# A hybrid decoder layer on one core: second expert list by column tiles, state-space copies on ScalarE and GpSimd, output projection begun in the gated unit

## The chip, the cores and the metric

The kernel runs on one core of a Trainium2 chip. The metric is the device time of one execution in microseconds (us), the median of several runs; one further execution was profiled. The engines are TensorE (PE, its weight loads PEld), VectorE (DVE), ScalarE (ACT), GpSimd (POOL) and the queue engine SyncE (SP).

## The reference

One layer works on 1024 prompt rows and 8 sample rows of width 1024: a modulated RMS norm, an input projection, then two branches side by side (gated delta rule with four heads, and a diagonal complex state space, "S5", with 32 groups of 16 channels and 64 states), one output projection over both, and a grouped top-2 mixture of 16 experts. What matters here, cut down:

```python
y, x_new = s5_scan(u, x0_s5, ...)            # x_t = Lbar x_{t-1} + Bbar u_t,  y_t = Re(C x_t) + D u_t
y = gelu(y)
y = y * sigmoid(y @ glu_w + glu_b)           # the gated unit
o_b = rms_norm(y, s5_norm_g)
out = concatenate([o_a, o_b], -1) @ w_out    # o_a: delta rule, 512 columns; o_b: 512 columns
x = x + gt1 * out
hn = rms_norm(x, norm2_g) * (1 + sc2) + sh2
# every row goes to two of 16 experts
act = silu(hn @ w_gate[e]) * (hn @ w_up[e]) * combine
x = x + gt2 * (act @ w_down[e])
```

## The kernel before

Every engine runs its own list of instructions, written out by hand; semaphores order them. `X.did(ins, name)` counts a step of engine X and `X.wait(eng, name)` lets another engine wait for it. A wait holds all that is behind it on its engine. The work goes through blocks; three of them are touched.

*State space* (pools `pe`, `act`, `dve`, `pool`, loops `for q in range(4)`, 8 groups in each quarter). The sequence is cut into chunks of 8 steps. For each quarter TensorE transposes the inputs V (`turn_rows`, to banks 2 and 3), the decode inputs (`turn_decode`) and the table W (step `BM`), makes the lag kernel K (step `K`, banks 4 and 5) and the state inputs (step `b`, from BM, BS and U, into banks 0 to 3). ScalarE copies U, Ud, BM and BS out of PSUM. VectorE builds the tables W, CL and CS (`tables`), copies K to Kt, adds the diagonal D to its lag 0 (`dd`), rotates the state inputs by the phases Ec and Es (L1767, step `rot`), runs the scan over chunks (L1826) and rotates back (step `zc`). GpSimd's part in a quarter is one addition to each half of zin, between rotation and scan. SP writes Kt eight times, shifted, into the block Toeplitz matrix TT (L1584); the output matmuls (step `yp`) wait for TT and `zc`. The modulation matmuls (`ada`) run between, in the banks of K.

*Gated unit and output projection*. `glu_tensor` transposes the nine row tiles of y, multiplies by glu_w (steps `glu0` to `glu8`, L1899; the ninth tile has 8 rows), and transposes the normed result (`turned`, L1889), which VectorE evicts into rows 4 to 7 of hT (`evict`, L1954). At i = 7 and 8 three of these transposes stand ahead of or behind a `glu` group. Six row transposes (`rowP`, L1910) are copied by ScalarE. Then the projection (L2648) goes over nine tiles in the order ORDER, two halves of 512 columns each, eight steps k of 128 in each half; steps 0 to 3 read the delta-rule half of hT, which is there since the block before. Routing of an earlier tile is placed between its matmuls (`route_T`, `route`).

*Experts*. Rows are sorted into slices of 64 for one expert; a tile holds two slices (LANES), which may belong to two experts. Expert 0 always has at least two slices. Three weight buffers are filled in turn, as soon as an expert is done (`moe_sync`); a fourth takes ScalarE's and VectorE's copy of the second lane's weights (`gate_up_copy`, `down_copy`). Which rows tile 1 takes is found by comparison (`hit1` on VectorE) and 18 products of the hits with the row numbers, summed in one PSUM column (`who1`, L2260; a float32 matmul is two instructions). GpSimd then gathers the rows (L2127). Tile 0's list (`who`, `who0`) is made earlier.

## Time and profile before

| | us |
|---|---|
| median of 3 runs (lowest, highest) | 1144.13 (1140.65, 1144.68) |
| the profiled execution, its own time | 1146.18 |
| its span in the trace | 1144.3 |
| TensorE busy | 1032.5 (90%) |
| VectorE busy | 582.6 (51%) |
| ScalarE busy | 355.6 (31%) |
| GpSimd busy | 222.8 (19%) |

Busy time is summed over the whole span; it doesn't say in which stage an engine is the one that the others wait for. Matmuls are pipelined, and their ends are modelled. In the lines of the trace, L1899 is line 1899 of the kernel, `out<-in` names the tiles, and a bracket tells how long the engine was idle before the instruction and what ended that.

### The profile page before, as it was taken

The page shows a single profiled execution, that of the slowest core. Times are in us where ns is not written, and L with a number is a line of the kernel's source. Part 1 is how long each engine was busy: PE and PEld are TensorE (multiplying, and loading weights), DVE is VectorE, ACT ScalarE, POOL GpSimd, SP SyncE. Part 2 cuts the span into 40 slices and gives each one's busy share as a digit, 9 for nine tenths or more (in the row PEclk, how much of TensorE's full clock was granted, in tenths as well). Part 3 has the DMA queues.
Part 4 walks back from the last instruction along what each step waited for, and adds up shares of the span by engine and source line. Part 5 has one row for each costly group of instructions (what it writes and reads, how often), then busy time and mean ns, then how long its engine had stood idle before and what let it go on. Part 6 is the DMA issues. An engine that isn't in the chain of part 4 may idle for free. (4 is left out here: it accounts for less than half of the span.)

```text
span 1144.3 us, 15471 instructions
## 1 busy us (share of the span) xinstructions
PE 1032.5 (90%) x5430; PEld 608.5 (53%) x5430; DVE 582.6 (51%) x1289; ACT 355.6 (31%) x723; POOL 222.8 (19%) x361
## 2 busy tenths in 40 slices
PE   3899999899999889969998889999669999999975
PEld 3466666444686777757886335344343333333332
DVE  3243436777236845669981432447653233332238
ACT  6121221115311454333223423332303333332333
POOL 0100000078150444320111000002132111111060
PEclk9899999899999887979988999999859999999988
DMA  9595434202000700058653510131527867699383
GB/s 334 191 241 197 194 115 179 74 38 88 28 13 26 150 2 1 2 178 284 202 199 131 221 74 19 61 106 38 173 67 262 305 229 260 227 352 360 119 316 133
DMA packets 126930, 177.07 MB, mean 155 GB/s; under 512 B 37406, under 2 KB 81683, under 8 KB 126840
## 3 DMA queue, kind: packets, MB, share of 16 engines
q1 hardware_dynamic: 117510, 147.03, 38.2%
q0 software_dynamic: 6432, 18.96, 4.7%
q10 hardware_dynamic: 2906, 10.02, 2.2%
q8 instruction: 47, 0.77, 0.3%
q14 instruction: 35, 0.29, 0.1%
HBM read 129.06 MB, written 45.85 MB: 153 GB/s over the span
## 5 line engine op out<-in xcount | busy, mean ns | idle before, releaser
L371 PE MATMUL bank<-hw 128*128 128x344 f32 x576 | 171.0, 459 | 3.8 <-ACT hw L555 3.8
L371 PEld LDWEIGHTS bank<-hw 128*128 128x128 f32 x576 | 110.6, 193 | 62.6 <-issue 6.4
L2215 PE MATMUL bank<-hw,H 128*64 (+1 forms) x608 | 135.7, 599 | 3.7 <-ACT hw L2293 2.2
L456 PE MATMUL bank<-hw 128*128 128x512 f32 x256 | 115.6, 609 | 4.3 <-ACT qkvT L583 4.3
L2648 PE MATMUL bank<-hw 128*128 128x512 f32 x256 | 116.8, 601 | 0.5 <-DVE hw L1954 0.5
L2215 PEld LDWEIGHTS bank<-hw,H 128*64 128x64 f32 x608 | 44.0, 139 | 91.4 <-issue 89.4
L456 PEld LDWEIGHTS bank<-hw 128*128 128x128 f32 x256 | 64.6, 256 | 51.0 <-issue 32.7
L2293 ACT ACTIVATE hw<-hw 128x2048 f32 (+1 forms) x21 | 40.0, 1909 | 127.2 <-PE bank L2215 92.9
L2233 PE MATMUL bank<-yy,H 128*64 128x512 f32 (+1 forms) x304 | 71.1, 611 | 2.1 <-ACT H L2272 2.1
L2648 PEld LDWEIGHTS bank<-hw 128*128 128x128 f32 x256 | 46.3, 190 | 49.8 <-issue 47.2
L2316 DVE COPY H<-bank 128x256 f32<-128x256 f32 x19 | 8.1, 424 | 113.7 <-PE bank L2198 113.7
L2127 POOL DMA_INDIRECT H<-h_d,small_room x20 | 21.3, 1065 | 193.6 <-DMA yy<-in_w_down 78.8
L577 ACT ACTIVATE pre<-bank 128x344 f32<-128x344 f32 x36 | 13.9, 459 | 122.9 <-PE bank L371 122.9
L915 DVE SCALAR_TENSOR_TENSOR qkvT<-pre,vecT,qkvT 128x1024 f32<-128x1024 f32 x36 | 46.0, 1279 | 0.0
L2432 PE MATMUL bank<-hw 128*128 128x512 f32 (+1 forms) x72 | 35.0, 635 | 8.7 <-DMA hw<-ys_d,pos 5.3
L2565 POOL DMA_INDIRECT ids_d<-small_room x18 | 18.3, 1017 | 124.4 <-DVE small_room L2834 103.9
L2233 PEld LDWEIGHTS bank<-yy,H 128*64 128x64 f32 x304 | 20.6, 139 | 39.1 <-issue 39.1
L908 DVE COPY tail<-pre 128x11 f32<-128x11 f32 x12 | 2.1, 173 | 71.1 <-ACT pre L577 71.0
L1899 PE MATMUL bank<-H,yy 128*128 128x512 f32 (+1 forms) x72 | 33.4, 625 | 0.3 <-DMA H<-in_s_glu_b 0.3
L700 POOL MEMSET V<- 128x8 f32 x2 | 0.2, 110 | 170.3 <-DVE V L892 170.3
L2293 ACT ACTIVATE yy<-yy 128x1024 f32 (+1 forms) x19 | 20.1, 1057 | 40.0 <-PE bank L2233 40.0
L2867 DVE TENSOR_TENSOR H<-bank,V 128x512 f32<-128x512 f32 x16 | 11.0, 690 | 36.5 <-PE bank L2648 36.5
(560 smaller groups left out, 1828.5 us busy)
## 6 DMA issues: line engine op xcount, KB each, us to landing
ys_d<-ZO SPq DMA_DIRECT2D x18, 1024.0 KB, 13.0
yy<-in_w_down SPq DMA_DIRECT2D x16, 1024.0 KB, 10.1
hw<-in_w_gate SPq DMA_DIRECT2D x16, 1024.0 KB, 7.1
hw<-in_w_up SPq DMA_DIRECT2D x16, 1024.0 KB, 10.6
ys_d<-H ACTq DMA_DIRECT2D x19, 512.0 KB, 6.3
hw<-in_w_in SPq DMA_DIRECT2D x4, 2048.0 KB, 8.1
yy<-in_w_ada SPq DMA_DIRECT2D x4, 2048.0 KB, 8.8
hw<-in_w_ada SPq DMA_DIRECT2D x8, 1024.0 KB, 12.1
```

Of the source, the lines that this page charges most:

```text
L371: mm = t.matmul(ps[3 * (m % 2) + s][:, 0:SEG], w_ring[:, q % 2, k, (m % 4) * P:(m % 4 + 1) * P], hT[:, k, s * SEG:(s + 1) * SEG], start=(k ...
L456: mm = t.matmul(ps[b % 4][0:n, :], tok, w_ring[:, q % 2, k, :], start=(k == 0), stop=(k == KD - 1))
L577: act.did(a.activation(pre[:, m % 2, 3 + s * SEG:3 + (s + 1) * SEG], ps[3 * (m % 2) + s][:, 0:SEG], ACT.Copy), f"pre{m}")
L915: dve.did(v.scalar_tensor_tensor(out=y, in0=pre[:, m % 2, i:i + SEQ], scalar=taps[i], in1=y, op0=ALU.mult, op1=ALU.add), f"conv{m}")
L1899: mm = t.matmul(ps[2 + i % 2][0:n, :], y1T[:, k, i * P:i * P + n], glu_w[:, k, :], start=(k == 0), stop=(k == 3))
L2127: g.indirect_dma_start(xin[s % 2][:, :], None, h2_d, bass.IndirectOffsetOnAxis(ap=who[s % 2][:, 0:1], axis=0)).then_inc(x_in[s % 2], 16)
L2215: mm = t.matmul(ps[2 + p][lane, :], xT[p][:, k, lane], wgu[:, bass.ds(bufs[j], 1), k, :].rearrange("p o n -> p (o n)"), start=(k == 0), st ...
L2233: mm = t.matmul(ps[5 + half_][lane, :], aT[s % 2][:, k, lane], wdn[:, bass.ds(bufs[j], 1), k, half_ * 512:(half_ + 1) * 512].rearrange("p ...
L2293: copy = lambda out, in_: a.activation(out, in_, ACT.Copy)
L2432: mm = t.matmul(ps[(5, 2)[i % 2] + half_][:, :], diag[0:n, i % 2, j, :], ya[i % YA][0:n, j, half_ * 512:(half_ + 1) * 512], start=(j == 0) ...
L2565: g.indirect_dma_start(ids_d, bass.IndirectOffsetOnAxis(ap=spot[0:n, i, j:j + 1], axis=0), ids[0:n, i:i + 1], None).then_inc(scat, 16)
L2648: mm = t.matmul(ps[b][:, :], hT[:, k, i * P:(i + 1) * P], w_out[:, k, cols], start=(k == 0), stop=(k == KD - 1))
```

## The change

Three edits. (1) State space: the two copies of K to Kt go from VectorE to ScalarE (new step `Kt`), the addition of the diagonal goes to GpSimd, which makes `dd` once for all groups; all that waited for VectorE's step `K` now waits for GpSimd's. In the first quarter ScalarE copies U as soon as the rows are transposed (new step `rows`), and TensorE does the state inputs (`state_inputs`) ahead of K. (2) Gated unit: `delta_half` does steps k = 0 to 3 of the first three half tiles of the projection in banks 0, 1 and 2, behind `glu7`, `glu8` and `G8`; the projection then goes on with k = 4 for these. (3) Experts: tile 0 takes expert 0's weights from buffer 0 for both lanes, and the copies for it go away; its transposes stand ahead of the second list; the list is made with the row numbers as weights (32 columns wide, the same number in each) on four column tiles and the hits as 128 moving columns, copied by ScalarE, and summed over the four by one more matmul.

```diff
@@ -1559,6 +1559,7 @@
         zl = t4("zl", [P, 2, GROUPS])
+        dd = t4("dd", [CH, GROUPS, CH])
         xrow = t4("xrow", [P, 2, P])
@@ -1575,7 +1576,7 @@
-                    dve.wait(sp, f"K{q}")
+                    pool.wait(sp, f"K{q}")
                     if q == 0:
@@ -1606,8 +1607,12 @@
                 pool.did(g.memset(zs[:, :, 0:1], 0.0), "clear")
+                pool.did(g.tensor_tensor(dd[:, :, :], bc(ident[0:CH, 0:CH], [CH, GROUPS, CH], 1), bc(D16[:, :], [CH, GROUPS, CH]), ALU.mult))
                 for q in range(4):
                     gs, Es = slice(q * NG, (q + 1) * NG), Es2[:, q % 2]
+                    act.wait(g, f"Kt{q}")
+                    pool.drain(g)
+                    pool.did(g.tensor_tensor(Kt[:, :, 0, :], Kt[:, :, 0, :], dd[:, gs, :], ALU.add), f"K{q}")
                     for bnk in range(2):
@@ -1623,8 +1628,9 @@
                     for x in range(NG):
-                        t.transpose(ps[2 + x // 4][:, (x % 4) * P:(x % 4 + 1) * P],
-                                    V[:, q * NG + x].rearrange("p j c -> p (j c)"), ident[:, :])
+                        mm = t.transpose(ps[2 + x // 4][:, (x % 4) * P:(x % 4 + 1) * P],
+                                         V[:, q * NG + x].rearrange("p j c -> p (j c)"), ident[:, :])
+                    pe.did(mm, f"rows{q}")
@@ -1646,6 +1652,15 @@
+                def state_inputs(q):
+                    act.wait(t, f"U{q}")
+                    for x in range(NG):
+                        if x % 4 == 0:
+                            act.wait(t, f"BM{q}_{x // 4}")
+                        t.matmul(ps[x // 4][:, (x % 4) * P:(x % 4 + 1) * P], BM[:, x, :], U[:, x, :], start=True, stop=True)
+                        mm = t.matmul(ps[2 + x // 4][:, (x % 4) * P:(x % 4 + 1) * P], BS[:, x, :], U[:, x, :], start=True, stop=True)
+                    pe.did(mm, f"b{q}")
+
                 turn_rows(0)
@@ -1655,6 +1670,7 @@
                         turn_decode(0)
+                        state_inputs(0)
                     else:
@@ -1662,13 +1678,8 @@
                     pe.did(mm, f"K{q}")
-                    act.wait(t, f"U{q}")
-                    for x in range(NG):
-                        if x % 4 == 0:
-                            act.wait(t, f"BM{q}_{x // 4}")
-                        t.matmul(ps[x // 4][:, (x % 4) * P:(x % 4 + 1) * P], BM[:, x, :], U[:, x, :], start=True, stop=True)
-                        mm = t.matmul(ps[2 + x // 4][:, (x % 4) * P:(x % 4 + 1) * P], BS[:, x, :], U[:, x, :], start=True, stop=True)
-                    pe.did(mm, f"b{q}")
+                    if q > 0:
+                        state_inputs(q)
                     dve.wait(t, "x0")
@@ -1684,7 +1695,7 @@
                         act.wait(t, f"yp{q - 1}")
-                    dve.wait(t, f"K{q}")
+                    pool.wait(t, f"K{q}")
                     if q == 0:
@@ -1699,7 +1710,7 @@
                     dve.wait(t, f"zc{q}")
-                    dve.wait(t, f"K{q}")
+                    pool.wait(t, f"K{q}")
                     t.wait_ge(tt_land, 16 * LAGS * (q + 1))
@@ -1724,11 +1735,12 @@
                 for q in range(4):
-                    pe.wait(a, f"U{q}")
+                    pe.wait(a, f"rows{q}")
                     if q > 0:
 ...
                         act.did(a.activation(U[:, 4 * bnk:4 * bnk + 4, :], ps[2 + bnk][:, :].rearrange("p (g n) -> p g n", g=4), ACT.Copy))
+                    pe.wait(a, f"U{q}")
                     act.did(a.activation(Ud[:, :, :, :].rearrange("p g v b -> p (g v b)"), ps[6][:, P:P + 2 * NG * DEC], ACT.Copy), f"U{q}")
@@ -1739,6 +1751,11 @@
                         act.did(a.activation(BS[:, part, ST:P], src[:, :, 0:ST], ACT.Copy, scale=-1.0), f"BM{q}_{bnk}")
+                    pe.wait(a, f"K{q}")
+                    if q > 0:
+                        a.wait_ge(tt_land, 16 * LAGS * q)
+                    for bnk in range(2):
+                        act.did(a.activation(Kt[:, 4 * bnk:4 * bnk + 4].rearrange("c g k n -> c (g k n)"), ps[4 + bnk][0:CH, :], ACT.Copy), f"Kt{q}")
                     pe.wait(a, f"x1_{q}")
@@ -1801,15 +1818,6 @@
                     gs, Ec, Es = slice(q * NG, (q + 1) * NG), Ec2[:, q % 2], Es2[:, q % 2]
-                    pe.wait(v, f"K{q}")
-                    if q > 0:
-                        v.wait_ge(tt_land, 16 * LAGS * q)
-                    for bnk in range(2):
-                        dve.did(v.tensor_copy(Kt[:, 4 * bnk:4 * bnk + 4].rearrange("c g k n -> c (g k n)"), ps[4 + bnk][0:CH, :]))
-                    sh = [CH, NG, CH]
-                    dd = Wt[0:CH, :, 0, :]
-                    tt(dd, bc(ident[0:CH, 0:CH], sh, 1), bc(D16[:, gs], sh), ALU.mult)
-                    tt(Kt[:, :, 0, :], Kt[:, :, 0, :], dd, ALU.add, f"K{q}")
                     if q < 3:
@@ -1889,6 +1897,12 @@
+            def delta_half(a, half_):
+
+                b, i, cols = 2 * a + half_, ORDER[a], slice(half_ * 512, (half_ + 1) * 512)
+                for k in range(4):
+                    t.matmul(ps[b][:, :], hT[:, k, i * P:(i + 1) * P], w_out[:, k, cols], start=(k == 0), stop=False)
+
             t.wait_ge(g_land, 32)
@@ -1899,8 +1913,14 @@
                 if i >= 7:
+                    if i == 7:
+                        gact.wait(t, "y1T8")
+                        t.wait_ge(land6, 48)
+                    delta_half(0, i - 7)
                     for j in range(3 * (i - 7), 3 * (i - 6)):
                         turned(j)
+            gdve.wait(t, "G8")
+            delta_half(1, 0)
             dve.wait(t, "A2")
@@ -2156,32 +2176,29 @@
-            return 0 if s == 0 else eng.value_load(slot_t[0:1, s, 1:2], min_val=0, max_val=BUFS - 1)
+            return eng.value_load(slot_t[0:1, s, 1:2], min_val=0, max_val=BUFS - 1)
 ...
             b = second(eng, s)
-            if s == 0:
-                eng.wait_ge(gu_in[0], 33)
-            else:
-                eng.wait_ge(gu_ready, s)
+            eng.wait_ge(gu_ready, s)
+            if s >= 2:
                 eng.wait_ge(gu_ps, s)
 ...
             b = second(eng, s)
-            if s == 0:
-                eng.wait_ge(dn_in[0], 17)
-            else:
-                eng.wait_ge(dn_ready, s)
+            eng.wait_ge(dn_ready, s)
+            if s >= 2:
                 eng.wait_ge(dn_ps, s)
 ...
-                first = 0 if s == 0 else t.value_load(slot_t[0:1, s, 0:1], min_val=0, max_val=BUFS - 1)
-                return first, BUFS
+                if s == 0:
+                    return 0, 0
+                return t.value_load(slot_t[0:1, s, 0:1], min_val=0, max_val=BUFS - 1), BUFS
@@ -2208,8 +2225,8 @@
                 for k in range(KD):
-                    if k % 4 == 0:
-                        t.wait_ge(gu_two[k // 4], s + 1)
+                    if s > 0 and k % 4 == 0:
+                        t.wait_ge(gu_two[k // 4], s)
                     for j in range(LANES):
@@ -2224,8 +2241,8 @@
                     t.wait_ge(dn_ready, s)
-                t.wait_ge(dn_two[0], s + 1)
-                t.wait_ge(dn_two[1], s + 1)
+                    t.wait_ge(dn_two[0], s)
+                    t.wait_ge(dn_two[1], s)
                 for half_ in range(2):
@@ -2253,13 +2270,15 @@
             pe.did(mm, "e_rows")
+            transposes(0)
             dve.wait(t, "hit1")
-            for j in range(2):
-                for i in range(9):
-                    n = P if i < NT else DEC
-                    mm = t.matmul(ps[4][:, 0:1], hit[0:n, 9 * j + i, :], ids_f[0:n, i:i + 1], start=(j == 0 and i == 0), stop=(j == 1 and i == 8))
-            pe.did(mm, "who1")
-            transposes(0)
+            for n in range(18):
+                lane, i = 32 * (n % 4), n % 9
+                rows = P if i < NT else DEC
+                mm = t.matmul(ps[4][lane:lane + 32, 0:P], ids_f[0:rows, i:i + 1].to_broadcast([rows, 32]), hit[0:rows, n, :], start=(n < 4), stop=(n >= 14))
+            pe.did(mm, "list1")
+            act.wait(t, "list1")
+            pe.did(t.matmul(ps[4][:, P:P + 1], lg_part[:, :], pick16[:, 0:1], start=True, stop=True), "who1")
             tiles(t, body, tail)
@@ -2281,8 +2300,8 @@
                 a.activation(sg[p][:, :], ps[2 + p][:, 0:FE], ACT.Silu).then_inc(silu_sb, 1)
-                down_copy(a, copy, 0, s)
                 if s > 0:
+                    down_copy(a, copy, 0, s)
                     out(s - 1)
@@ -2291,8 +2310,8 @@
             copy = lambda out, in_: a.activation(out, in_, ACT.Copy)
-            for n in range(2):
-                gate_up_copy(a, copy, n, 0)
+            pe.wait(a, "list1")
+            act.did(a.activation(lg_part[:, :], ps[4][:, 0:P], ACT.Copy), "list1")
             a.wait_ge(h2_out, 16 * 9)
@@ -2321,9 +2340,9 @@
                         dve.did(v.tensor_tensor(hit[:, 9 * j:9 * j + 9, :], bc(ps[6][:, 0:P], [P, 9, P], 1), bc(col[:, 5 + j, :], [P, 9, P]), ALU.is_equal), "hit1")
+                    x_copy(0)
                     pe.wait(v, "who1")
-                    dve.did(v.tensor_copy(who[1][:, :], ps[4][:, 0:1]), "who1")
-                    x_copy(0)
+                    dve.did(v.tensor_copy(who[1][:, :], ps[4][:, P:P + 1]), "who1")
                     expert_rows(v)
@@ -2335,7 +2354,8 @@
                 v.tensor_tensor(hh_[p][:, :], sg[p][:, :], ps[2 + p][:, FE:2 * FE], ALU.mult).then_inc(h_sb, 1)
-                down_copy(v, v.tensor_copy, 1, s)
+                if s > 0:
+                    down_copy(v, v.tensor_copy, 1, s)
             tiles(v, body, a_copy)
@@ -2643,13 +2663,13 @@
                             dve.wait(t, f"mix{ORDER[a - 2]}_{half_}")
-                        for k in range(KD):
+                        for k in range(4 if 2 * a + half_ < 3 else 0, KD):
                             if i < NT:
 ...
                                 mm = t.matmul(ps[b][j:j + 32, :], hT[:, k, T - 32:T], w_out[:, k, cols], start=(k < 4), stop=(k >= 4))
-                            if a in BESIDE and (half_, k) == (0, 3):
+                            if a in BESIDE and (half_, k) == ((0, 3) if a > 1 else (0, 4)):
                                 route_T(t, BESIDE[a])
 ...
                                     ranks(t, a - 6)
```

## Rows read from the trace of the kernel before

**Rows 1.** The page's busy time, share of the span and instructions of each engine
```profile
PE 1032.5 (90%) x5430; PEld 608.5 (53%) x5430; DVE 582.6 (51%) x1289; ACT 355.6 (31%) x723; POOL 222.8 (19%) x361
```

**Rows 2.** Busy time by stage: from:to us, length, engines, granted clock, DMA share, GB/s
```profile
518.00:520.00 2.00, 2.00 (x10) 2.00 (x11) 1.97 (x4) 0.00 (x0) 0.00 (x0) 0.54 1.05 394
...
578.00:585.00 7.00, 7.00 (x38) 6.98 (x37) 6.65 (x7) 0.00 (x0) 0.00 (x0) 0.52 1.05 396
...
649.00:653.00 4.00, 3.88 (x10) 1.37 (x8) 1.54 (x4) 2.67 (x5) 0.00 (x0) 1.00 0.00 0
...
653.00:659.00 6.00, 2.16 (x13) 1.63 (x14) 5.67 (x11) 2.81 (x5) 0.00 (x0) 0.78 0.00 1
...
659.00:665.00 6.00, 6.00 (x13) 1.21 (x12) 0.32 (x1) 0.00 (x0) 0.00 (x0) 0.65 0.00 0
...
676.00:814.00 138.00, 136.11 (x553) 64.93 (x554) 65.02 (x173) 41.17 (x75) 12.91 (x14) 1.00 0.14 50
...
836.00:839.00 3.00, 0.48 (x6) 0.19 (x5) 2.62 (x2) 0.00 (x0) 2.10 (x3) 0.50 0.08 7
```

**Rows 3.** The chain that ended last, gated unit to projection: start us, us, what
```profile
659.02 5.64 PE bank L1899 x8
...
665.96 1.93 DVE hw L1954 x2
...
673.69 0.45 PE bank L1889 x4
...
676.24 7.13 PE bank L2648 x16
```

**Rows 4.** The same chain before and in the first expert tiles
```profile
838.99 8.11 PE bank L2260 x36
...
850.50 9.00 PE bank L2215 x32
...
860.52 1.92 ACT hw L2293
```

**Rows 5.** VectorE's timeline in the state space: start us, us, operation, [idle before]
```profile
518.68 1.27 DVE L1808 COPY Kt<-bank 16x512 f32<-16x512 f32 x2
...
522.69 0.69 DVE L1767 TENSOR_TENSOR hw<-bank,Ec 128x512 f32<-128x512 f32 x1 [1.98 <-PE bank L1670]
...
525.57 3.67 DVE L1826 TENSOR_TENSOR_SCAN zs<-small_room,hw 128x128 f32<-128x128 f32 x8
...
545.70 0.69 DVE L1767 TENSOR_TENSOR hw<-bank,Ec 128x512 f32<-128x512 f32 x1
```

**Rows 6.** TensorE's timeline, state space and routing of the last tile
```profile
514.37 3.60 PE L1662 MATMUL bank<-CL,small_room 128*16 128x128 f32 x16 [0.54 <-DVE CL L1767]
...
545.26 0.39 PE L1670 MATMUL bank<-hw 128*128 128x128 f32 x2
...
817.04 0.64 PE L2597 MATMUL bank<-V,yy 128*32 128x128 f32 x16 [0.78 <-DVE small L2877]
```

**Rows 7.** ScalarE's timeline, state space and routing in the projection
```profile
513.86 1.08 ACT L1731 ACTIVATE hw<-bank 128x512 f32<-128x512 f32 x2 [7.91 <-PE bank L1636]
...
515.73 0.43 ACT L1741 ACTIVATE hw<-bank 128x256 f32<-128x256 f32 x1
...
707.33 0.28 ACT L2718 ACTIVATE small_room<-bank 128x128 f32<-128x128 f32 x1 [6.06 <-PE bank L2597]
```

**Rows 8.** GpSimd's timeline, state space and start of the next block
```profile
510.33 1.25 POOL L1606 TENSOR_TENSOR pick<-pick,ident 128x9 f32<-128x9 f32 x1
...
524.18 1.28 POOL L1614 TENSOR_TENSOR hw<-hw 128x512 f32<-128x512 f32 x1 [11.66 <-DVE hw L1767]
...
618.88 0.22 POOL L2529 TENSOR_TENSOR small_room<-small_room,ident 128x16 f32<-128x16 f32 x1
```

**Rows 9.** SP's timeline: Kt transfers of the first quarter, a late weight load
```profile
520.60 6.46 SPq L1584 DMA_DIRECT2D hw<-Kt  x8
...
1021.81 0.37 SPq L2019 DMA_DIRECT2D hw<-in_w_gate  x1
```

## The prediction

> **What bounds the kernel now.** The busy times come first [rows 1]: TensorE works 1032.5 of 1144.3 us, VectorE half of it, so time comes back only where TensorE waits or works at half clock. The table by stage [rows 2] finds such places around the change: in 653 to 659 us (gated unit) TensorE works 2.16 of 6 us, in 659 to 665 it is busy but its granted clock is 0.65, and in 836 to 839 (before the experts) it works 0.48 of 3 us at 0.50. In the output projection, 676 to 814, it works 136.11 of 138 us at full clock: work moved out of there shortens it. The chain of waits says what sets the gaps: in the gated unit VectorE's evictions and the small last matmul group [rows 3]; before the experts the 36 matmuls of the second list, 8.11 us [rows 4]. The state space (506 to 617 us) has no piece in the printed chain, so there I read one engine's timeline after the other [rows 5 to 8].
>
> **The state space (four quarters of 8 groups).** Off VectorE go two copies of Kt (1.27 us) and two small operations behind them: in the first quarter that work, with a small decode copy that stays, fills 518.68 to 520.71 (522.69 less the idle 1.98), about 1.9 us, 7.6 over four quarters. But the next large operation is the rotation, and it waits for the state inputs on TensorE: those 1.98 us of idleness [rows 5]. In the second quarter the rotation starts at 545.70, while TensorE's last state input starts at 545.26 and takes 0.39, to 545.65 [rows 5, 6]: nothing was lost to Kt there either. So VectorE's relief alone is worth next to nothing; for all quarters I put 0.15.
>
> The reordering touches the first quarter alone. ScalarE copies U (1.08 us from 513.86) before the decode transposes and not after them, so its BM copies come some 0.95 earlier: the first four groups are ready at 515.1, not 516.1 [rows 7]. TensorE's state inputs then start at 515.1; before, they stood behind K, which took 3.60 us at half clock until 518.0 [rows 6]. They ended some 0.3 before the rotation's 522.69, and the clock rose at about 519.8 (0.54 over 518 to 520, [rows 2]): 1.9 us at half clock and 2.6 at full, or 3.5 at full clock. With the clock up at 520.0 they now end at 521.0 (4.9 at half clock, 1.0 at full), and the rotation could start at 521.3, 1.4 earlier. K follows, half of 3.60, to 522.8.
> But GpSimd now has to add the diagonal to Kt *ahead* of its additions to zin, in its own order, and VectorE's scan waits for zin. Behind K come ScalarE's copies of Kt (no row has 16x512; nearest are two of 128x512 in 1.08, [rows 7]), to 524.0, the addition, and zin, 1.28 us. The addition of 16x128 lies between 0.22 (128x16) and 1.28 (128x512) [rows 8]; by elements 0.46. So the scan starts at 525.8, where it started at 525.57 [rows 5]: the gain is gone, and 0.2 with it. The Kt transfers start 4 us later too; SP's eight issues take 6.46 us [rows 9], so they end near 531 and land after it, about when the scan's results are there: between nothing and 0.8 us more for TensorE, of which I take half. Loss 0.6, less 0.15: **0.5 us**. Ends: the clock rises only after these matmuls, K ends 2.5 later, loss 3; it rises 2 us sooner, gain 1.2. In the other quarters K, its copy and its addition come before the rotation, and nothing queues. One thing may go either way: TensorE runs 578 to 585 at 0.52 [rows 2], 3.5 us that a slightly shifted order may win or pay once more.
>
> On GpSimd a 128x9 addition took 1.25 us beside VectorE's tables, a larger one (128x16) 0.22 with VectorE nearly idle [rows 8]. The Trainium skill (SBUF — State Buffer, Who interferes with whom) has the rule for it: GpSimd and a VectorE tensor_tensor with both inputs in SBUF hold one pair of ports by turns, each for a whole instruction. By the rule the first quarter's addition to Kt runs free (the rotation reads PSUM), and the later ones wait a table operation, about 1.2 us, on slack; were the first held once, the loss would be 1.7.
>
> **The gated unit and the projection.** Three half tiles do four of their eight steps earlier: 24 instructions of 0.43 (16 in 6.9, [rows 3]), 10.3 us off the projection. Their weights are there: from 649 to 659 next to nothing moves on the DMA engines [rows 2], so land6 costs nothing. The cover is the gap after the eighth matmul group, which ends at 652.9 (3.88 busy of 649 to 653). I walk it.
> *First half tile*: 652.9 to 656.3. Transposes 0 and 1 follow (0.45 each and more, [rows 3]) to 657.4, transpose 2 to 658.5, after an eviction; these evictions come 0.2 late. The last, narrow group (glu8) took 5.64 us from 659.02, since the clock had dropped in the gap [rows 2, 3]; with TensorE busy through it I take full clock, 8 x 0.43 = 3.4, to 661.9: 2.7 sooner.
> *Second half tile*: to 665.4, ahead of transposes 3 to 5. Evictions resumed 1.3 after glu8 (664.66 to 665.96) and took 1.93 for two [rows 3]; now the first runs 663.2 to 664.2, but the second waits for transpose 3, 666.0 to 666.95: 0.9 before its old end, 667.89.
> *Third half tile*: after transposes 4 and 5, 667.5 to 671.0. Six groups of row transposes alternate with ScalarE's copies (0.54 each): 3.5, to 674.5; before, the first of the last three transposes stood at 673.69 and the projection began 2.55 later [rows 3], so now at 677.1, 0.9 late. Early in it the transposes of the first tile wait some 0.3 for VectorE, as fewer matmuls stand ahead. Gain 10.3 - 0.9 - 0.3 = **9.1 us**. Ends: glu8 and the second half tile at half clock, 2.2 and 3.4 less, 3.5; all hidden, 10.3.
>
> **The start of the experts.** The 36 matmuls with one moving column become 36 on four column tiles of 32; the row of that shape is 16 in 0.64 at full clock [rows 6], so 1.4, and 2.7 at the 0.50 granted here. Added behind: a 128x128 copy by ScalarE, 0.28 [rows 7], a small matmul, at most 0.4, and 0.2 of handing over. Moved off the path: the transposes of tile 0 and VectorE's copies of them, which filled 847.1 (end of the list) to 850.5; they now run beside `hit1` and the list. They wait for the gather of tile 0, which has landed: in 836 to 839 the engines move 7 GB/s [rows 2]. So the list takes 838.99 to 841.7, and tile 0's gate-up starts at 842.55, not 850.50 [rows 4]: **8.0 us**. Ends: the four tiles not side by side, 1.2 less; the list at full clock, 1.3 more; gate-up too (9.00 us, 2 of it from the low clock), 2 more. The dropped copies of expert 0's weights lie in ScalarE's idle time before the list or behind the gate-up: nothing. ScalarE's copy for tile 1 (1.92 at 860.52, [rows 4]) still waits for the end of tile 0's gate-up, so that stall stays. Tile 1's gather is issued by POOL behind the list as before, 8 us sooner.
> Behind it all is called by use: SP issues a weight load at 1021.81 [rows 9], in the moment when a gate-up ends. So the shift goes through to the end.
>
> **Sum.** +0.5 - 9.1 - 8.0 = -16.6. The profiled execution took 1146.2 us (span 1144.3 and 1.9 around it), so 1129.6; the median of the runs lies 2.1 below it: **1127.5**.
>
> **Rivals.**
> 1. *Gap filled, clock not held*: glu8 and the second half tile at half clock, 5.6 less: 1133. For it: 578 to 585, at half clock though busy; against: four wide matmuls stand in front. 0.12.
> 2. *Tile 0's transposes block the list*: they stand ahead of it and wait for the gather; were it to land at 842, list and gate-up come 4 to 5 later: 1132. Against: the quiet engines at 836. 0.06.
> 3. *The weight stream sets the end*, and what gated unit and experts give is lost again: 1144. For it: TensorE's waits near the end; against: each load is issued upon use [rows 9]. 0.05.
> 4. *GpSimd's order, the other side*: the addition to Kt ahead of zin holds every scan. It decides from 4.2 us a quarter (16.6 over four); at 6 us a quarter the time is 1151. For it: the first quarter, where I find 0.2; against: in the others K ends before the state inputs start. 0.03.
> 5. *VectorE's relief counts in full*: 7 us more gain, 1120. Against: [rows 5, 6]. 0.03.
>
> **How the numbers follow.** Forecast 0.71. Its own ends reach from 1122 to 1132; rivals 1, 2 and 5 and the 3.5 us of clock widen that to 1120 to 1136, which leaves out rivals 3 and 4 and the tails. About 0.5% (5.7 us) is what a measurement of this kernel tells from no change. Faster: forecast, 1, 2 (nearly all) and 5, 0.91; same: 3 and a rest of 2, 0.06; slower: 4, 0.03.
>
> **What would show it.** Right: no copy of Kt on VectorE, yet from the second quarter on rotations within 0.5 us of before, counted from the stage's start; the first scan waiting for GpSimd; glu8 near 3.4 us; the projection under 130 us; a list under 3 us, tile 0's gate-up some 4 us after `hit1`, and ScalarE's copy still between the first two gate-ups. Wrong: glu8 again over 5 us; a wait for the gather ahead of the list; the last expert ending where it did.

## The result and the profile after

| | before | after |
|---|---|---|
| median (lowest, highest), 5 runs each, us | 1144.34 (1140.65, 1145.48) | 1133.48 (1127.33, 1135.04) |
| ratio, 95% interval | | 0.9895 [0.9873, 0.9917] |
| the profiled execution and its span | 1146.18, 1144.3 | 1127.33, 1125.6 |

The changed kernel is 10.9 us faster by the medians, 12.0 by the ratio. The median was forecast at 1127.5; 1133.48 is inside the range and 6.0 above the forecast. A second measurement of the same program, with other runs (e5 below), gave 0.9853 [0.9834, 0.9871], 16.9 us. All nine executions of the changed kernel together have a median of 1130.58 us, 14.4 below the 1144.9 of the 57 executions of the kernel before.

The stages first, each cut out of PE's and SP's timelines at the same events in both kernels (us):

| stretch | before | after | gain |
|---|---|---|---|
| start to SP's first load of Ec (the state space begins) | 506.27 | 504.73 | 1.54 |
| to SP's load of glu_w (the state space ends) | 111.43 | 111.31 | 0.12 |
| to the first matmul of the projection's loop | 58.54 | 59.87 | -1.33 |
| to the last matmul of that loop | 137.85 | 128.09 | 9.76 |
| to tile 0's gate-up | 36.41 | 29.00 | 7.41 |
| to tile 1's gate-up | 12.17 | 11.57 | 0.60 |
| to the end | 281.63 | 281.03 | 0.60 |

The first line lies before all edits; over all the profiles of this study it goes from 502.2 to 506.4 us, so its 1.54 belongs to the execution, not to the change. What the edits gave is in the four lines behind it, 16.0 us; the 0.60 of tile 0's gate-up is the clock's, as is shown below, and the 0.60 at the end lies behind all edits.

The page's busy times, for [rows 1]: VectorE gives up 6.7 us, TensorE 8.9, with two instructions more.

```profile
PE 1023.6 (91%) x5432; PEld 603.1 (54%) x5432; DVE 575.9 (51%) x1272; ACT 355.0 (32%) x729; POOL 225.3 (20%) x366
```

The table by stage, for [rows 2], same columns:

```profile
578.00:585.00 7.00, 7.00 (x89) 6.82 (x88) 6.71 (x6) 1.01 (x7) 0.00 (x0) 1.00 1.05 396
...
653.00:659.00 6.00, 5.18 (x22) 2.26 (x21) 4.00 (x8) 1.05 (x3) 0.00 (x0) 1.00 0.00 0
659.00:665.00 6.00, 5.88 (x20) 2.48 (x18) 2.79 (x4) 1.35 (x3) 0.00 (x0) 1.00 0.57 187
676.00:814.00 138.00, 130.78 (x566) 64.17 (x566) 72.65 (x200) 44.13 (x81) 12.91 (x14) 0.98 0.20 69
```

TensorE works 5.18 of the 6 us from 653 (2.16 before) and the clock stays at its upper level, where it fell to 0.78 and 0.65 before. The stretch 578 to 585, at 0.52 before, is at 1.00 too; that looks like a gain of the state-space edit, and the experiments show that it is none.

TensorE's timeline of the gated unit, for [rows 3]; L1904 are the moved steps, L1913 the `glu` groups, L1897 the transposes of the result, L1930 the row transposes, L2668 the projection:

```profile
650.93 3.60 PE L1904 MATMUL bank<-hw 128*128 128x512 f32 x8
654.36 1.04 PE L1897 MATMUL bank<-ident,yy 128*128 128x128 f32 x8
656.22 0.63 PE L1897 MATMUL bank<-ident,yy 128*128 128x128 f32 x4 [0.82 <-DVE hw L1974]
656.78 3.60 PE L1913 MATMUL bank<-H,yy 128*8 128x512 f32 x8
...
660.31 3.70 PE L1904 MATMUL bank<-hw 128*128 128x512 f32 x8
663.85 1.04 PE L1897 MATMUL bank<-ident,yy 128*128 128x128 f32 x8
665.70 0.63 PE L1897 MATMUL bank<-ident,yy 128*128 128x128 f32 x4 [0.82 <-DVE hw L1974]
666.17 3.60 PE L1904 MATMUL bank<-hw 128*128 128x512 f32 x8
669.60 1.04 PE L1930 MATMUL bank<-ident,modT 128*128 128x128 f32 x8
670.89 1.14 PE L1930 MATMUL bank<-ident,small_room 128*128 128x128 f32 x8 [0.25 <-ACT V L1958]
672.23 1.14 PE L1930 MATMUL bank<-ident,modT 128*128 128x128 f32 x8 [0.20 <-ACT V L1958]
...
675.06 0.38 PE L1897 MATMUL bank<-ident,yy 8*128 8x8 f32 x4 [0.82 <-DVE hw L1974]
675.91 1.55 PE L2668 MATMUL bank<-hw 128*128 128x512 f32 x3 [0.47 <-DVE hw L1974]
```

The ninth group (L1913, 8 rows) takes 3.60 us where it took 5.64, and the order is the one that the prediction walked.

TensorE's timeline before the experts, for [rows 4]; L2209 are tile 0's transposes, L2278 the list, L2281 its sum, L2232 the gate-ups:

```profile
826.51 1.97 PE L2209 MATMUL bank<-ident,H 128*128 128x128 f32 x8
828.89 3.22 PE L2278 MATMUL bank<-yy,small_room 128*32 128x128 f32 x36 [0.41 <-DVE yy L2342]
832.48 0.59 PE L2281 MATMUL bank<-small_room 128*128 128x1 f32 x2 [0.37 <-ACT small_room L2314]
833.00 8.43 PE L2232 MATMUL bank<-hw,H 128*64 128x512 f32 x32
...
844.57 7.09 PE L2232 MATMUL bank<-hw,H 128*64 x32 [2.12 <-ACT hw L2312]
```

The list takes 3.22 us where it took 8.11, the transposes stand where VectorE makes the hits, and ScalarE's copy still holds tile 1 for 2.12 us.

The first quarter of the state space, for [rows 5, 6, 8, 9], by the timelines of TensorE (K), VectorE, GpSimd and SP.

```profile
519.67 1.92 PE L1678 MATMUL bank<-CL,small_room 128*16 128x128 f32 x16
```

```profile
519.78 0.69 DVE L1784 TENSOR_TENSOR hw<-bank,Ec 128x512 f32<-128x512 f32 x1 [1.70 <-PE bank L1661]
...
524.55 3.63 DVE L1834 TENSOR_TENSOR_SCAN zs<-small_room,hw 128x128 f32<-128x128 f32 x8 [1.90 <-POOL hw L1619]
```

```profile
522.77 0.44 POOL L1615 TENSOR_TENSOR Kt<-Kt,dd 16x128 f32<-16x128 f32 x1 [10.48 <-ACT Kt L1758]
523.18 2.50 POOL L1619 TENSOR_TENSOR hw<-hw 128x512 f32<-128x512 f32 x2
```

```profile
523.24 5.70 SPq L1585 DMA_DIRECT2D hw<-Kt  x8
```

From the stage's start (506.27 before, 504.73 after) the rotation comes at 15.05 us, not 16.42, as forecast 1.4 earlier; the scan comes at 19.82, not 19.30. GpSimd stands between: its addition to zin can't start before the diagonal is added. What TensorE waits for next, its output matmuls of this quarter, comes 0.48 us later, at 26.11 instead of 25.63. The first line is the kernel before, the second the changed one:

```profile
531.90 0.46 PE L1706 MATMUL bank<-hw 128*128 128x128 f32 x2 [1.09 <-issue]
...
530.84 0.46 PE L1717 MATMUL bank<-hw 128*128 128x128 f32 x2 [1.23 <-DVE zl L1841]
```

### The profile page after: what moved, and what is told of

Same layout as the page of the kernel before. It is cut to its first block and busy times, and to the rows that moved or that the text cites. A ratio compares the mean times of both kernels' runs of the same rounds, so it can differ in the third digit from the quotient of the medians.

```text
span 1125.6 us, 15469 instructions
## 1 busy us (share of the span) xinstructions
PE 1023.6 (91%) x5432; PEld 603.1 (54%) x5432; DVE 575.9 (51%) x1272; ACT 355.0 (32%) x729; POOL 225.3 (20%) x366
## 5 line engine op out<-in xcount | busy, mean ns | idle before, releaser
L371 PEld LDWEIGHTS bank<-hw 128*128 128x128 f32 x576 | 109.8, 191 | 62.0 <-issue 5.4
L2232 PE MATMUL bank<-hw,H 128*64 (+1 forms) x608 | 135.1, 597 | 2.1 <-ACT hw L2312 2.1
L456 PE MATMUL bank<-hw 128*128 128x512 f32 x256 | 114.7, 605 | 4.3 <-ACT qkvT L583 4.3
L2668 PE MATMUL bank<-hw 128*128 128x512 f32 x232 | 106.5, 602 | 0.5 <-DVE hw L1974 0.5
L2232 PEld LDWEIGHTS bank<-hw,H 128*64 128x64 f32 x608 | 44.0, 138 | 88.9 <-issue 88.9
L456 PEld LDWEIGHTS bank<-hw 128*128 128x128 f32 x256 | 64.2, 254 | 50.5 <-issue 32.1
L2312 ACT ACTIVATE hw<-hw 128x2048 f32 x19 | 36.3, 1911 | 109.1 <-PE bank L2232 90.2
L2668 PEld LDWEIGHTS bank<-hw 128*128 128x128 f32 x232 | 41.7, 190 | 44.1 <-issue 41.5
L1913 PE MATMUL bank<-H,yy 128*128 128x512 f32 (+1 forms) x72 | 31.3, 594 | 0.1
L2312 ACT ACTIVATE yy<-yy 128x1024 f32 x18 | 19.0, 1058 | 37.7 <-PE bank L2250 37.7
L2452 PEld LDWEIGHTS bank<-hw 128*128 128x128 f32 (+1 forms) x72 | 14.0, 203 | 28.8 <-issue 19.9
## 6 DMA issues: line engine op xcount, KB each, us to landing
hw<-in_w_up SPq DMA_DIRECT2D x16, 1024.0 KB, 10.9
```

What stands on the lines that cost most here:

```text
L371: mm = t.matmul(ps[3 * (m % 2) + s][:, 0:SEG], w_ring[:, q % 2, k, (m % 4) * P:(m % 4 + 1) * P], hT[:, k, s * SEG:(s + 1) * SEG], start=(k ...
L456: mm = t.matmul(ps[b % 4][0:n, :], tok, w_ring[:, q % 2, k, :], start=(k == 0), stop=(k == KD - 1))
L1913: mm = t.matmul(ps[2 + i % 2][0:n, :], y1T[:, k, i * P:i * P + n], glu_w[:, k, :], start=(k == 0), stop=(k == 3))
L2232: mm = t.matmul(ps[2 + p][lane, :], xT[p][:, k, lane], wgu[:, bass.ds(bufs[j], 1), k, :].rearrange("p o n -> p (o n)"), start=(k == 0), st ...
L2312: copy = lambda out, in_: a.activation(out, in_, ACT.Copy)
L2452: mm = t.matmul(ps[(5, 2)[i % 2] + half_][:, :], diag[0:n, i % 2, j, :], ya[i % YA][0:n, j, half_ * 512:(half_ + 1) * 512], start=(j == 0) ...
```

## The experiments

The theory: the time comes from two places, 9 us in gated unit and projection and 8 before the experts, and the state-space edit gives nothing, because TensorE and GpSimd, not VectorE, set that stage. Rivals: the gains don't add; the state-space edit costs time in company with the others; the clock in the gap has another cause than the idleness there. All ratios are to the kernel before on the same chip.

**One edit alone, and two without the third.** Each kernel takes the hunks of the change's diff that belong to its edits, and no others; the marks of each:

```diff
# e1: L1559 to L1829 only
-                    pe.wait(v, f"K{q}")
+                    pe.wait(a, f"K{q}")
# e2: L1889 to L1914 and L2643 to L2652 only
+                    delta_half(0, i - 7)
# e3: L2156 to L2338 only
+            pe.did(mm, "list1")
# e4, e6: the last two
```

> Only the state-space edit on the kernel before. My theory: VectorE waits for the state inputs with or without its copies, and the first scan now waits for GpSimd, so the time stays within 3 us of before (ratio 0.998 to 1.003). Rival 1 (VectorE's relief counts): 5 to 7 us faster, 0.994 to 0.995. Rival 2 (the moved copies and the new order cost TensorE clock or order, which would explain that the whole change gave 11 us and its profiled execution 19): 4 to 6 us slower, 1.004 to 1.005.

> Only the three half tiles of the projection moved into the gated unit. My theory: 8 to 9 us faster, ratio 0.992 to 0.993, the ninth matmul group of the gated unit (8 rows) near 3.5 us. Rival (the clock drops there in most executions): 3 to 5 us faster, that group again above 5 us.

> Only the experts' edit: second list by column tiles behind the first transposes, no weight copies for tile 0. My theory: 7.5 to 8.5 us faster, ratio 0.9925 to 0.9935, and the last expert ends earlier by the same. Rival (later weight loads and gathers swallow it): under 3 us faster, with the waits of the last experts longer than before by the difference.

> The whole change without its state-space edit. My theory: the two other edits add, 16 to 17 us faster, ratio 0.985 to 0.986, and this is as fast as the whole change or up to 1 us faster. Rival (state-space edit costs 4 to 6 us in most executions): the same 16 to 17 us here, clearly faster than the whole change's 0.9895. Rival 2 (the edits don't add in the median): about 11 us, 0.990, like the whole change.

| | median, us | ratio [95%] | difference by the ratio, us |
|---|---|---|---|
| e1 state space alone | 1145.83 | 1.0009 [0.9992, 1.0026] | +1.0 |
| e2 projection alone | 1135.66 | 0.9919 [0.9890, 0.9949] | -9.3 |
| e3 second list alone | 1137.78 | 0.9936 [0.9912, 0.9960] | -7.3 |
| e4 the last two | 1125.36 | 0.9826 [0.9796, 0.9855] | -19.9 |

The parts sum to -15.6, and the state-space edit alone shows no gain: the interval leaves it between 0.9 us of gain and 3 of loss. The other three fall outside what was expected of them: 9.3 against 8 to 9, 7.3 against 7.5 to 8.5, and e4's 19.9 against 16 to 17. In the traces e2 has the projection at 128.07 us and its start at 59.81 after the load of glu_w, as the whole has; e3 has 28.96 us from the projection to tile 0's gate-up. But e4 stood 9 us below the first measurement of the whole, which left a rival: that the state-space edit costs something beside the others. So both went on one chip, in one set of runs:

> The whole change once more, beside the next two on one chip. State-space edit alone measured 1.0009 and the other two edits together 0.9826. If the three edits add, 0.9835 (19 us faster). Rival: together with the others the state-space edit costs 6 to 8 us, 0.989 to 0.990 as measured first.

> The whole change without its state-space edit, as partner of the run before. If edits add: within 0.002 of the whole change. Rival (cost of the state-space edit in company): 0.006 to 0.007 below it.

The whole took 1128.57 us, 0.9853 [0.9834, 0.9871], and the two edits without the state space 1129.49, 0.9861 [0.9841, 0.9881]. The two intervals all but coincide, so the cost of 6 to 8 us that the rival asks for is not there. Two things more follow from these runs. e4 and e6 are one program, at 1125.36 and 1129.49 us, and the first measurement and e5 are another, at 1133.48 and 1128.57. The intervals of the last two, [0.9873, 0.9917] and [0.9834, 0.9871], don't even overlap: a set of runs can be off by 4 or 5 us, more than its own interval says. A difference of that size between edits is not shown by times alone, which is why the traces decide below.

**Why VectorE's relief gives nothing.** VectorE's timeline gives the start of each quarter's rotation, counted from the stage's start (us):

| | 1st | 2nd | 3rd | 4th |
|---|---|---|---|---|
| before | 16.42 | 39.43 | 62.64 | 88.50 |
| e3 (this stage as before) | 16.03 | 40.17 | 63.38 | 86.45 |
| after | 15.05 | 41.04 | 64.11 | 87.17 |
| e5 (the same program) | 15.59 | 40.41 | 63.47 | 87.87 |

A quarter without a fall of the clock lasts 23.0 to 23.2 us in either form (23.01, 23.21 before; 23.07, 23.06 after). Some are longer because TensorE is at its lower level for some us: 25.86 in the third before, 24.14 in the first of e3 (granted clock 0.66 in 531 to 536 us), 24.40 in the third of e5. Which quarter it is changes between e3 and before, whose stage is the same code, and between after and e5, which are one program. The clear stretch 578 to 585 above is therefore no gain: in the changed kernel the fall lies in 531 to 536 (0.66 too). The first quarter with the edit is longer for another reason besides. In e5 it lasts 24.82 us without any fall (1.00 throughout 517 to 543): its rotation came earlier, and TensorE's work behind it did not. In after, 25.99, both reasons meet: 1.1 us for the fall, as in e3, and some 1.85 for the earlier rotation. With the edit the stage lasted 111.25 to 111.31 us in five profiles (110.69 in e12, whose order in the first quarter is another), without it 110.21 to 111.43 in eight. VectorE's freed time shows as a wait for the state inputs before every rotation of the changed kernel, 1.69 to 3.11 us; the longest:

```profile
545.77 0.69 DVE L1784 TENSOR_TENSOR hw<-bank,Ec 128x512 f32<-128x512 f32 x1 [3.11 <-PE bank L1661]
```

**The order in the first quarter.** First the old order of TensorE and ScalarE there, with the copies still off VectorE:

```diff
                     if q == 0:
                         turn_decode(0)
-                        state_inputs(0)
...
-                    if q > 0:
-                        state_inputs(q)
+                    state_inputs(q)
...
-                    pe.wait(a, f"rows{q}")
+                    pe.wait(a, f"U{q}")
```

> The whole change, but in the first quarter K stands ahead of the state inputs again and ScalarE copies U behind the decode transposes; the copies of Kt stay with ScalarE and GpSimd. My theory: the new order gains nothing, since GpSimd's addition to Kt stands ahead of its additions to zin; so the time is that of the whole change within 2 us, the first scan no longer waits for GpSimd's Kt, and the rotation is about 2 us later. Rival (the order is what costs): 4 us or more faster than the whole change. Rival 2 (the order gains): 2 us or more slower.

It took 1131.62 us, 0.9874 [0.9853, 0.9894]; the interval overlaps that of e5, so the time decides nothing. VectorE and GpSimd in e7:

```profile
522.11 0.69 DVE L1782 TENSOR_TENSOR hw<-bank,Ec 128x512 f32<-128x512 f32 x1 [3.45 <-PE bank L1661]
...
524.98 3.68 DVE L1832 TENSOR_TENSOR_SCAN zs<-small_room,hw 128x128 f32<-128x128 f32 x8
```

```profile
518.91 0.44 POOL L1615 TENSOR_TENSOR Kt<-Kt,dd 16x128 f32<-16x128 f32 x1 [6.05 <-ACT Kt L1756]
523.60 1.27 POOL L1619 TENSOR_TENSOR hw<-hw 128x512 f32<-128x512 f32 x1 [4.25 <-DVE hw L1782]
```

The stage began at 505.30: rotation at 16.81 us, scan at 19.68, against 15.05 and 19.82 in the whole. In the old order the rotation is 1.8 us later and the scan no later, because GpSimd has added the diagonal 4.7 us before. So the new order does win at the rotation, and GpSimd's queue takes it. But e7's rotation is also 0.39 us later than the 16.42 of the kernel before, whose order it has: K waits for VectorE's table CL until 8.84 us into the stage, not 8.10, because GpSimd's product for `dd` holds up that table (see the rule on the ports below). The other way round, GpSimd's first addition to zin goes ahead:

```diff
+                def diagonal(q):
+                    gs = slice(q * NG, (q + 1) * NG)
                     act.wait(g, f"Kt{q}")
                     pool.drain(g)
                     pool.did(g.tensor_tensor(Kt[:, :, 0, :], Kt[:, :, 0, :], dd[:, gs, :], ALU.add), f"K{q}")
...
+                    if q > 0:
+                        diagonal(q)
                     for bnk in range(2):
...
                         pool.did(g.tensor_tensor(zin[:, part], zin[:, part], z2[:, part], ALU.add), f"zin{q}_{bnk}")
+                        if q == 0 and bnk == 0:
+                            diagonal(q)
```

> The changed kernel, with GpSimd's first addition to zin ahead of the addition of the diagonal in the first quarter. My theory: the scan of the first quarter starts about 1.8 us earlier (18.0 instead of 19.8 us from the stage's start), since GpSimd's order held it, but the output matmuls of the quarter then wait for the transfers of Kt to TT, which start about 1.0 us later and take 5.7 to issue: they start within 0.5 us of the changed kernel or up to 1.0 later, and the stage's length stays at 111.3 within 1. Rival (the scan alone decides): the output matmuls start 1.8 us earlier and the stage is 1.5 or more shorter.

1130.90 us, 0.9883 [0.9849, 0.9918]: no faster. VectorE's scan in e12 and TensorE's output matmuls:

```profile
521.59 4.08 DVE L1841 TENSOR_TENSOR_SCAN zs<-small_room,hw 128x128 f32<-128x128 f32 x8
...
521.93 1.84 DVE L1841 TENSOR_TENSOR_SCAN zs<-small_room,hw 128x128 f32<-128x128 f32 x1
```

```profile
529.77 0.46 PE L1724 MATMUL bank<-hw 128*128 128x128 f32 x2 [1.24 <-DMA hw<-Kt]
```

The stage began at 503.12, so the scan starts at 18.47 instead of 19.82 us: 1.35 earlier, 1.8 expected. One of its eight steps takes 1.84 us; of that below. The output matmuls start at 26.65, against 26.11 in the whole (530.84 less 504.73), and what they wait for is no longer VectorE but the transfers of Kt, whose issue SP begins at 19.16 instead of 18.51. The fairer partner is e5, the whole in an execution whose first rotation comes at 15.59 us as in e12. TensorE's output matmuls in e5, whose stage began at 502.17:

```profile
528.80 0.46 PE L1717 MATMUL bank<-hw 128*128 128x128 f32 x2 [1.22 <-DVE zl L1841]
```

They start at 26.63, no later than in e12, although the scan of e5 starts at 20.34, 1.87 later. Whichever addition GpSimd does first, the other is late for the output matmuls: the rival, that the scan alone decides, falls. The order is not quite without worth: VectorE's tables for the second quarter come sooner too, and its rotation starts at 39.96 in e12, at 40.41 in e5, with no fall of the clock before it in either. Whether these 0.45 us reach the end no run shows.

**What the idle gap in the gated unit costs.** The kernel before, with eight matmul instructions that nobody reads in the gap behind the eighth group; the projection is as before:

```diff
                 gpe.did(mm, f"glu{i}")
                 if i >= 7:
+                    if i == 7:
+                        gact.wait(t, "y1T8")
+                        for k in range(4):
+                            t.matmul(ps[0][:, :], y1T[:, k, 0:P], glu_w[:, k, :], start=(k == 0), stop=(k == 3))
```

> The kernel before with eight matmul instructions whose product nobody reads, put into TensorE's gap behind the eighth group of the gated unit. If the ninth group (8 rows) was slow because the clock had dropped in that gap, it now takes 3.4 to 3.6 us, where it took 5.64, and the projection starts about 2 us sooner after the gated unit's start, though TensorE does more. Rival (the group is slow for its shape of 8 rows): 5.6 us as before.

One run, 1144.06 us. TensorE's timeline in it (L1905 the unread matmuls, L1899 the ninth group, L1914 the row transposes):

```profile
652.51 3.60 PE L1905 MATMUL bank<-H,yy 128*128 128x512 f32 x8
...
658.35 3.60 PE L1899 MATMUL bank<-H,yy 128*8 128x512 f32 x8
...
668.51 1.97 PE L1914 MATMUL bank<-ident,small_room 128*128 128x128 f32 x8 [1.25 <-ACT V L1942]
```

With matmuls in the gap the ninth group takes 3.60 instead of 5.64 us, and the granted clock is 1.00 in 653 to 665: the group's length was the clock's, not that of its 8 rows, and without the gap the clock didn't fall there. But it fell later. TensorE waits again, 1.86 and 1.25 us, and in 665 to 675 the clock is 0.66, so the row transposes take 1.97 us for eight. In the kernel before they ran at the upper level:

```profile
671.22 1.14 PE L1910 MATMUL bank<-ident,small_room 128*128 128x128 f32 x8 [1.68 <-ACT V L1938]
```

The projection therefore starts 57.94 us after the load of glu_w, where it started at 58.54: 0.6 sooner, not the 2 us that were expected. In this one execution the filling moved the fall instead of removing it. In the changed kernel the second and third half tile stand in those places, and no fall follows.

**The third half tile spread.** The brackets of the gated unit after still show TensorE waiting 0.25, 0.20, 0.82 and 0.47 us. Its four steps are taken apart:

```diff
-            delta_half(1, 0)
...
             for b in range(6):
+                if b == 2:
+                    third_half(0, 3)         # steps k = 0 to 2
...
             for i in range(6, 9):
+                if i == 8:
+                    third_half(3, 4)         # step k = 3
                 turned(i)
```

> The changed kernel, with the four steps of the third half tile of the projection taken apart: the row transposes 0 and 1 in front, three steps behind them while ScalarE loads a table and copies, the fourth step between the last transposes of the gated unit. In the changed kernel TensorE stands idle in 666 to 676 us for 0.25, 0.20, 0.82 and 0.47 us there, and the row transposes run at ScalarE's pace. My theory: the projection starts 0.7 to 1.1 us earlier, counted from the end of the second half tile, and the end comes as much earlier; time ratio to the changed kernel 0.999, which only the trace can show. Rival (the waits are for VectorE's normalized rows, not for ScalarE): no change of the start of the projection. Rival (the clock falls in a new gap): later.

1129.35 us, 0.9875 [0.9845, 0.9906]. The time can't tell it from the whole; the trace can. TensorE in e11 (L1936 row transposes, L1909 the spread steps, L2676 the projection):

```profile
666.16 1.04 PE L1936 MATMUL bank<-ident,modT 128*128 128x128 f32 x8
667.04 2.74 PE L1909 MATMUL bank<-hw 128*128 128x512 f32 x6
...
672.75 1.02 PE L1909 MATMUL bank<-hw 128*128 128x512 f32 x2
673.74 0.38 PE L1897 MATMUL bank<-ident,yy 8*128 8x8 f32 x4
674.60 3.70 PE L2676 MATMUL bank<-hw 128*128 128x512 f32 x8 [0.47 <-DVE hw L1982]
```

The projection starts 14.30 us behind the second half tile, 15.60 in the whole: 1.30 earlier, more than the 0.7 to 1.1 expected. Two of the waits are gone, and 128.08 us of projection follow, as in the whole.

**The second list in halves.** The move of the transposes alone, and the column tiles alone:

```diff
# e9
+            transposes(0)
             dve.wait(t, "hit1")
...
             pe.did(mm, "who1")
-            transposes(0)
...
+                    x_copy(0)                # VectorE
                     pe.wait(v, "who1")
...
-                    x_copy(0)
# e10: the new list, ScalarE's copy and the sum; transposes(0) stays behind them
```

> The kernel before, with the transposes of tile 0 and VectorE's copies of them ahead of the old 36-matmul list; list, order of weights and copies as before. My theory: the part of the third edit that comes from the move. The list then starts about 2.4 to 2.9 us after the transposes began, as before, takes 8.1 us again, and tile 0's gate-up starts right behind it: from the list's start to the gate-up 8.1 instead of 11.5 us, 3.4 us of gain, ratio about 0.997. Rival (the transposes wait for the gather of tile 0): the list starts 4 or more us later than 3 us after the transposes of the hits row, gain 0 or less. Rival (gains overlap, the list alone would have hidden the transposes): gain under 1.5.

> The kernel before, with the new list on four column tiles, ScalarE's copy and the last small matmul, but the transposes of tile 0 behind it as before, and expert 0's weights still copied to the fourth buffer. My theory: the list takes 3.2 us and 1.2 of copy, hand-over and summing matmul, 4.4 instead of 8.1, so the time from its start to the gate-up falls from 11.5 to about 7.8 us, 3.7 of gain, ratio about 0.997; with the other half 7.1, which is what the third edit gave by itself. Rival (clock: the short list is followed by transposes at half clock and the time is given back): gain under 2. Rival (ScalarE, which still has two copies of 1.9 us of weights in front of the list copy, is late): the copy starts more than 0.5 us behind the list.

e9: 1141.21 us, 0.9976 [0.9953, 1.0000]; e10: 1141.04, 0.9966 [0.9946, 0.9986]. The trace has the halves apart. From the list's start to tile 0's gate-up it was 11.51 us before; in e9 it is 8.03, in e10 7.49. TensorE in e9:

```profile
834.43 1.97 PE L2192 MATMUL bank<-ident,H 128*128 128x128 f32 x8 [0.27 <-DMA H<-h_d,small_room]
836.69 8.10 PE L2261 MATMUL bank<-small_room,yy 128*128 128x1 f32 x36 [0.29 <-DVE yy L2323]
844.72 8.97 PE L2215 MATMUL bank<-hw,H 128*64 128x512 f32 x32
```

and in e10:

```profile
838.82 3.22 PE L2260 MATMUL bank<-yy,small_room 128*32 128x128 f32 x36 [2.52 <-DVE yy L2327]
842.40 0.58 PE L2263 MATMUL bank<-small_room 128*128 128x1 f32 x2 [0.37 <-ACT small_room L2299]
```

The move is worth 3.48 us (3.4 expected), the new list 4.02 (3.7 expected); together 7.50, about what the whole shows between projection and gate-up (7.41). Dropping the copies of expert 0's weights, which e9 and e10 keep, adds nothing to that. In e9 the transposes waited 0.27 us for the gather, and so they did in the changed kernel itself, in e5:

```profile
824.60 1.97 PE L2209 MATMUL bank<-ident,H 128*128 128x128 f32 x8 [0.27 <-DMA H<-h_d,small_room]
```

It was 0.23 to 0.43 us in e4, e6, e7, e11 and e12, and no wait shows in after and e3. So the gather has nothing to spare; mostly it costs nothing, since the list behind it still waits for `hit1` (0.28 us in e5), but in e12, with 0.43, the list no longer waits.

## Why the prediction was right, and where its sizes were off

**State space**, forecast a loss of 0.5: 0.6 in the first quarter, less 0.15 for VectorE's relief. Measured alone +1.0 with an interval of -0.9 to +3.0. The stage's length, 111.27 us in the mean of five profiles with the edit and 110.88 in the eight without it, doesn't settle it either: the eight differ among themselves by 1.2 us, though their stage is one code. The cleanest reading is the output matmuls of the first quarter, ahead of every fall: in the two profiled executions the clock rises 13.5 us into the stage, and these matmuls come 0.48 us later than before, where the prediction took 0.6. From the second to the third rotation VectorE's relief saves 0.15 us (23.06 in e5, 23.21 before), as much as was put for all quarters together. The steps came as walked: rotation 1.4 us earlier, scan waiting for GpSimd (1.90 us), the diagonal's addition 0.44 where 0.46 was put. One reading was off without harm: the state inputs of the kernel before end 0.04 us before the rotation (522.26 and 0.39), not 0.3. GpSimd's order holds the first scan only (rival 4 falls): from rotation to scan 4.77 us there, 2.80 or 2.81 in the other quarters, as before. One test that the prediction named failed: rotations of later quarters within 0.5 us of before. They differ by 1.3 to 1.6 us. The second comes 1.6 later, of which 1.1 is the fall of the clock in that place and the rest the late output matmuls; the fourth comes 1.3 earlier, since the kernel before has its fall ahead of it. The length of a quarter at the upper level, 23.0 to 23.2 in either form, is what bears out that VectorE's relief gives next to nothing.

**Gated unit and projection**, forecast 9.1. Trace 8.4 (9.76 less 1.33), e2 alone 9.3. The loop gave 9.76, forecast 10.3 less 0.3 of waiting; the term that was mis-sized most is the late start, 1.33 against 0.9. In the gated unit TensorE waits for VectorE's evictions 0.82 us three times and for ScalarE's copies 0.25 and 0.20; with another order of the same work, in e11, the projection starts 1.30 us sooner. The clock held, so rival 1 (glu8 at 5.6 us) falls.

**Experts**, forecast 8.0. Trace 7.41 to tile 0's gate-up and 0.60 more to tile 1's; e3 alone 7.3. The list took 3.22 us, not 2.7, the mis-sized term: 36 instructions at 0.089 us each, in a stretch at the lower clock (0.50 in 829 to 832), where the row that priced it gave 0.040 at full clock. Part of it is the sum itself: twice the 1.4 of full clock is 2.9 (36 by 0.040 by 2), not 2.7. The test of a list under 3 us failed with it. The 0.60 is in the gate-up of tile 0, 8.43 us instead of 8.97; e3, with the same edit, has 9.29 there and e6 7.09, so it is the clock's and no effect of the edit. The working's sentence that the gather of tile 0 has landed did not hold in every execution: the wait that it named as a sign of being wrong is there, but with 0.23 to 0.43 us it is a tenth of what rival 2 asks for; rival 3 (the weight stream) falls, since tile 1's gate-up to the end took 281.0 us against 281.6; rival 5 falls with e1.

By the stages, then, the sum was 16.0 us where 16.6 was forecast, and both gains came out smaller than forecast, by 0.7 and 0.6. That the two sums lie so close is in part luck: in the two profiled executions the state space shows a gain of 0.12 where its first quarter shows a loss. With the 0.5 of loss that was forecast in its place the sum is 15.3. That the first median shows 10.9 is not in any edit: the second measurement of the same program shows 16.9. The two sets differ in TensorE's mean granted clock. The first set's fastest execution, the one that was profiled, had 0.944 and a span of 1125.6 us; its other four had 0.935 to 0.938. The second set had 0.939 to 0.944. The kernel before shows the same tie: of all its executions here, those at 1137 to 1140 us had 0.940 to 0.943 and those at 1148 to 1149 us 0.932 to 0.938. This is an agreement of two numbers, not an experiment, and what makes one execution's clock lower than another's stays open: only one execution of each set was profiled. The working took no account of it, except as 3.5 us for one stretch of the state space.

**The rule on the ports** (the Trainium skill, SBUF — State Buffer, Who interferes with whom: GpSimd and a VectorE operation with both inputs in SBUF hold a pair of ports by turns). The trace bears it out in two places. Beside GpSimd's product for `dd`, VectorE's sum for CL takes 2.09 us, where the other three take 1.36, as do all four in the kernel before; the prediction had no term for this.

```profile
511.42 2.09 DVE L1784 TENSOR_TENSOR CL<-CL,Wt 128x1152 f32<-128x1152 f32 x1
...
537.40 1.36 DVE L1784 TENSOR_TENSOR CL<-CL,Wt 128x1152 f32<-128x1152 f32 x1
```

VectorE's scan shows it too. Beside GpSimd's second addition to zin, which ends at 525.68, the first of eight steps takes 1.42 us, where a step otherwise takes 0.39; in e12 the second step takes 1.84 from 521.93, and GpSimd's additions run until 523.49.

```profile
524.55 1.42 DVE L1834 TENSOR_TENSOR_SCAN zs<-small_room,hw 128x128 f32<-128x128 f32 x1 [1.90 <-POOL hw L1619]
```

The additions to Kt, 0.44 to 0.48 us in all quarters, met no such hold: they begin 0.07 to 0.08 us behind ScalarE's copy, when VectorE's last table is over or about to end (in the third quarter that table starts at 565.53 and takes 1.23, the addition starts at 566.59). The 1.2 us that the prediction gave by that rule were not seen.

## What to carry to other kernels

An engine's relief is worth only what the others waited for it *last*: VectorE gave up 6.7 us of work, and in the changed kernel every rotation behind it waits for TensorE instead. When an engine has one queue, an operation moved to it stands ahead of something; find out which transfer and which engine wait for each order, since here either order on GpSimd made the other side late. Work that is ready early pays twice when it fills a gap behind which the clock fell; see that the fall doesn't come back in the next gap, as it did in e8. And where the clock wanders, one median is not enough, nor is its interval: two sets of runs of one program lay 5 us apart here. Read the stages of the traces, and compare executions in which the clock falls in the same places.

## What the runs showed of the hardware

- The stretch in which TensorE falls to its lower level in the state space wanders from execution to execution between the quarters, with the same code (e3 and before, after and e5), and costs 1.1 (e3's first quarter, 24.14 against 23.01 us) to 2.9 us (before's third, 25.86) in a quarter.
- Float32 matmuls with one moving column and 128 weight columns took 0.225 us an instruction at a granted clock of 0.5 (8.11 for 36); with 32 weight columns and 128 moving ones, on four column tiles, 0.089 (3.22 for 36).
- In every quarter of the changed kernel one step of the scan takes 1.4 us instead of 0.39, the first one beside GpSimd's addition to zin; the longest of the 32 steps takes 1.441 us there and 1.444 in the kernel before. No edit here touches that.
- Filling one gap moved the fall of the clock to a later one: in the kernel before the granted clock is 0.78 and 0.65 in 653 to 659 and 659 to 665 us and 1.00 in 665 to 676; in e8 it is 1.00 in 653 to 665 and 0.66 in 665 to 675.
